# Branch weights moved forward in the sync queue of a hybrid decoder layer with a mixture of experts

## What is computed

```python
xn = rms_norm(x, attn_norm_g)
q, k, v, qi, ki, wi, u, ga, gb = split(xn @ w_in)
attn_o = sparse_attention(...)            # indexer picks keys; sample tokens read paged caches
pool_o = pool_branch(u, ...)
m = sigmoid(ga) * (attn_o @ w_branch_attn) + sigmoid(gb) * (pool_o @ w_branch_pool)
h = x + m @ w_out
h = h + moe_ffn(rms_norm(h, ffn_norm_g))  # 32 experts, each with gate, up and down weights
y = rms_norm(h, final_norm_g)
```

## Time and profile before

| | us |
|---|---|
| three runs | 1102.05, 1099.07, 1102.0; median 1102.0 |
| profiled execution | 1100.63 |
| span in its profile | 1099.1 |
| PE busy | 943.1 (86%) |
| DVE busy | 340.9 (31%) |
| ACT busy | 202.2 (18%) |
| POOL busy | 197.9 (18%) |
| mean DMA rate over the span | 258 GB/s |

### The profile page before, as it was taken

One profiled execution on the slowest core, in us unless ns is written; L12 is line 12 of the kernel. 1 busy time (PEld: TensorE's weight loads), 2 busy tenths in 40 slices (PEclk: granted clock), 3 DMA queues, 4 the chain that ended last, 5 costly groups with the idle time before them and its releaser, 6 DMA issues.

```text
span 1099.1 us, 12164 instructions
## 1 busy us (share of the span) xinstructions
PE 943.1 (86%) x4705; PEld 532.2 (48%) x4705; DVE 340.9 (31%) x756; ACT 202.2 (18%) x446; POOL 197.9 (18%) x296
## 2 busy tenths in 40 slices
PE   7978999999999998999994999888778887878870
PEld 6634444767776656774552434434334242442420
DVE  2269999973441111331226000100000000000016
ACT  3243110213343424000220110000000000000012
POOL 2730660100001110000132111111111111111122
PEclk9989999999999999999996999999999999999995
DMA  9920212512202545933027999999999999999985
GB/s 337 392 86 1 77 47 76 183 53 77 77 1 89 218 154 164 335 149 153 19 96 283 413 421 422 421 423 425 423 422 425 422 425 421 424 425 424 419 320 188
DMA packets 53402, 283.82 MB, mean 258 GB/s; under 512 B 8652, under 2 KB 9520, under 8 KB 32999
## 3 DMA queue, kind: packets, MB, share of 16 engines
q1 hardware_dynamic: 42519, 246.24, 55.8%
q0 software_dynamic: 10784, 36.97, 9.3%
q10 hardware_dynamic: 56, 0.01, 0.0%
HBM read 267.41 MB, written 23.17 MB: 264 GB/s over the span
## 4 chain that ended last, share of the span: by engine, by line
PE 47%; DMA 29%; DVE 18%; ACT 2%; issue 2%; SPq 1%; POOL 0%; ACTq 0%; POOLq 0%; DVEq 0%; PEldq 0%
DMA arena<-in_w_exp_up 24%; PE psum L798 9%; DVE arena L1442 6%; DVE arena L1440 6%; PE psum L952 5%; PE psum L1038 5%; PE psum L934 4%; PE psum L1035 4%; PE psum L1036 3%; PE psum L1053 3%; DMA arena<-in_w_branch_pool 3%; PE psum L622 3%; PE psum L886 1%; DMA y_d<-arena 1%; PE psum L634 1%
## 5 line engine op out<-in xcount | busy, mean ns | idle before, releaser
L1038 PE MATMUL psum<-arena 128*64 128x512 f32 x704 | 169.1, 636 | 30.5 <-DMA arena<-in_w_exp_up 29.8
L1053 PE MATMUL psum<-arena 128*64 128x512 f32 x512 | 116.9, 597 | 17.7 <-ACT arena L1335 17.7
L798 PE MATMUL psum<-arena 128*128 128x288 f32 x480 | 126.1, 416 | 0.0
L1038 PEld LDWEIGHTS psum<-arena 128*64 128x64 f32 x704 | 55.7, 146 | 142.1 <-issue 108.1
L798 PEld LDWEIGHTS psum<-arena 128*128 128x128 f32 x480 | 89.6, 192 | 31.0 <-issue 8.1
L1679 DVE TENSOR_TENSOR arena<-arena,psum 128x256 f32<-128x256 f32 x32 | 13.5, 421 | 277.3 <-ACT arena L1331 277.3
L608 PE MATMUL psum<-arena 128*128 128x512 f32 x192 | 86.2, 604 | 2.1 <-ACT arena L1202 2.1
L1331 ACT ACTIVATE arena<-psum 128x256 f32<-128x256 f32 x32 | 12.3, 383 | 405.1 <-PE psum L1038 277.1
L1053 PEld LDWEIGHTS psum<-arena 128*64 128x64 f32 x512 | 40.4, 136 | 72.1 <-issue 71.4
L1687 DVE COPY arena<-psum 128x512 f32<-128x512 f32 x31 | 21.4, 691 | 152.2 <-PE psum L1053 152.2
L1440 DVE MAX8 arena<-arena 64x8 f32<-64x1032 f32 (+3 forms) x80 | 66.2, 828 | 2.8
(11 more groups left out here) (279 smaller groups left out, 1021.4 us busy)
## 6 DMA issues: line engine op xcount, KB each, us to landing
arena<-in_w_exp_down SPq DMA_DIRECT2D x32, 2048.0 KB, 37.0
arena<-in_w_exp_gate SPq DMA_DIRECT2D x30, 2048.0 KB, 32.7
arena<-in_w_exp_up SPq DMA_DIRECT2D x20, 2048.0 KB, 37.2
arena<-in_w_exp_up SPq DMA_DIRECT2D x24, 1024.0 KB, 34.6
arena<-in_w_in SPq DMA_DIRECT2D x7, 2048.0 KB, 8.7
y_d<-arena SPq DMA_DIRECT2D x1, 8192.0 KB
arena<-in_x_prompt SPq DMA_DIRECT2D x8, 512.0 KB, 7.0
arena<-in_w_out SPq DMA_DIRECT2D x2, 2048.0 KB, 10.9
```

The source lines that it names most:

```text
L798: last = pe.matmul(bank(2 + n % 2 if n < SAMPLE_G else 2, HN), ring[slot % 2][:, k, m * P:(m + 1) * P], xnT[:, k, HN * hh:HN * hh + HN], s ...
L1038: last = pe.matmul(bank(2 + s, 512, rows).rearrange("p (w n) -> p w n", w=2), x_k, wgu[j][:, :, DE * k + 256 * q:DE * k + 256 * q + 256], ...
L1053: last = pe.matmul(bank(4 + s, 512, slice(64 * half, 64 * half + 64)), hT[s][:, k % 2, CAP * (k // 2):CAP * (k // 2) + CAP], wd[j][:, k, 5 ...
```

## The change

Block 7 is issued before the wait for the attention, with only its own wait (`g_done` 24) ahead of it. Block 8 takes the place behind `att_all` and `stores_done`, ahead of the residual's rows, the router's weights and expert 0, where it waits for `g_done` 32. It is taken out from behind expert 0. Nothing else is changed: the other four engines have the same instructions in the same order.

```diff
             for n in range(4, 7):
                 load_ring(n)
 
+            load_ring(7)
             sp.wait_ge(S["att_all"], 1)
             stores_done(sp)
-            load_ring(7)
+            load_ring(8)
             sp.wait_ge(S["gs_done"], len(gb_raw))
             for i in range(TILES):
                 sp.dma_start(resid[0:rows_of(i), i, :], x_rows[i]).then_inc(s_res, 16)
...
             load_gate_up(0, 0)
             load_down(0, 0)
-            load_ring(8)
             sp.dma_start(flat(wg2), g_v[2]).then_inc(s_gu[2], 16)
             load_ring(9)
             load_ring(10)
```

## The result

| | before | after |
|---|---|---|
| median of five runs, us | 1099.75 (1098.78 to 1102.05) | 1094.42 (1092.54 to 1094.63) |
| ratio, 95% interval | | 0.9944 (0.9930 to 0.9958) |
| span in the profile, us | 1099.1 | 1090.9 |
| first L927 to first L952, us | 75.81 | 71.17 |

The changed kernel is faster by 0.56%, with an interval of 0.42 to 0.70%; the medians are 5.3 us apart. The forecast was 4.1 us (0.37%), and 1097.2 us: the direction was right, the measured time lies at the low edge of the range, and the forecast gain lies outside the interval of the ratio.

What follows compares the result with a forecast made beforehand. No engine was taken to bound the whole span (chain 47% PE, 29% DMA, 18% DVE). Two waits, -1.8 - 2.3 = -4.1 us, gave 1097.2 us, the middle of 1096.5 and 1097.9; range 1094.0 to 1100.5.

Steps and rivals of the forecast that it cites:

- Both waits go: PE's idle time before the two branch halves, 1.80 us for block 7 and 2.31 us for block 8, disappears.
- its 442 to 456: Bounds in us for the landing of the moved block 8, which PE wants at 463.8.
- The sum, -1.8 - 2.3: The waits for block 7 and block 8 before the branch halves go, together -4.1 us.
- The upper bound of the forecast, 4.3: Largest gain, -4.3 us: PE's instruction groups overlap by 0.1 us where nothing waits, two times.
- its rivals: Experts swallow the gain, 0.09; only block 7 helps, 0.03; gathers late, kernel slower, 0.03; SP late to block 7, 0.02.
- Block 7 beside the gathers, cost 0: Block 7's 2.1 MB run beside the attention's gathers from 357; cost 0 to 0.5 us, taken as 0.
- the lower bound: Gathers and block 7 share 390 GB/s: values there at 367.1, keys at 372.5, both early, cost 0.
- The upper bound (block 7 whole and first, keys 8.1 us later): Block 7 takes 9.8 us first: values at 372.1, 0.5 us late; keys at 378.5, in time.
- The row that I leaned on: Profile row of DMA slices: in every full slice of a gather the engines reach 344 GB/s and more.
- a gather late by 5.4 us: Estimate for the value gather beside block 7, 2.1 MB at 390 GB/s, within its slack of 9.3 us.
- Everything behind block 8 on SP has room: Residual's rows, router's weights and expert 0 go out 6.9 us later, block 9 comes behind; cost 0.
- The gain is kept by the experts: The expert weights' stream starts and ends as much earlier as PE, so the 4.1 us stay.

Runs made afterwards that it cites:

- the stops: Changed kernel with seven stops of PE put into the branch products: long stops (about 2 us) 1110.91 us, short stops (about 0.5 us) 1099.65 us.
- its repetition: The changed kernel once more with no edit, against the kernel before on the same chip: 1094.04 us, ratio 0.9950.
- block 8 alone: Kernel before with only block 8 moved, to right after block 7, which stays behind the wait for the attention: 1097.35 us, ratio 0.9973.
- block 7 alone twice: Kernel before with only block 7 moved ahead of the attention's wait, profiled twice: 1098.62 us, ratio 0.9987.
- the one with more traffic: Changed kernel with two more transfers of 2 MB issued right behind block 7: 1099.52 us.
- the one with the rest held longer: Changed kernel with residual's rows, router's weights, expert 0 and expert 2's gate weights held until 8 of 32 branch products are done: 1092.82 us, ratio 0.9933.
- the three further profiles: The kernel before, unedited, profiled three more times on another chip: L927 to L952 took 79.72, 76.26 and 76.28 us.

## Why the prediction was right in its mechanism and short in its size

**Both waits go.** Right, in every profile of the changed kernel. Block 8's last transfer was issued at 433.01 and landed 8.4 us later, at 441.4; L927 came 2.2 us earlier than in the kernel before, so this is 443.6 by the forecast's clock, near the lower end of its 442 to 456.

**The sum, -1.8 - 2.3.** This is the step that failed. The mechanism was right and the term was mis-sized: I took the idle time ahead of two instructions, in one execution, for the whole price of a wait. Taken from five profiles of the kernel before and, for the restart, from the stops, the price of the two waits has three parts. The idle time is 2.00 + 2.48 = 4.48 us. The restart is 2 x 0.27 = 0.54 us, which also stands in the first pair of profiles: 2 x 31.31 - 62.08. The clock falls behind four of ten waits, for 1.7 us each: 0.4 x 2 x 1.7 = 1.36 us. Together 6.4 us, and the direct difference of the stretch is 77.50 - 71.17 = 6.3 us. The third part is the least certain, since it comes from two executions of five. The timed runs agree: the mean of the changed kernel's eleven runs (the first five and the six of its repetition) is 1094.07, that of the 53 runs of the kernel before that stood beside the changed ones is 1099.92, so 5.9 us, with a 95% interval of about 0.8 to either side. That excludes the 4.1 of the forecast, and the 4.6 that the first pair of profiles gives. The upper bound of the forecast, 4.3, had taken the overlap of 0.1 us where nothing waits, but neither the full restart nor a granted clock that can fall, since both waits of the one profile stood at 1.00. The forecast named the granted clock nowhere in its rivals. The time itself, 1097.2, had a second error of 1.4 us: it stands on a kernel before of 1101.3 us (1097.2 + 4.1), taken from three runs and one profile, where the 53 runs give 1099.92.

**Block 7 beside the gathers, cost 0.** PE had no new wait there, so the cost was 0, but the delay of the keys was misjudged. The value gather landed at most 9.1 us after its issue instead of 8.0, so the load hardly touched it. The key gather landed after at most 13.0 instead of 7.6 us, 5.4 us later; the lower bound had allowed 2.1 us. The upper bound (block 7 whole and first, keys 8.1 us later) held. The row that I leaned on, the full slices of a gather, is not the rate that this load moves at. Slices of 1 us from 350 to 390 us in the changed kernel, which answer to the earlier trace rows:

```profile
GB/s 0 0 0 115 180 393 369 352 383 385 256 215 234 215 231 324 395 475 356 473 389 401 152 14 0 66 246 401 393 360 393 205 41 16 221 401 410 262 377 311
```

From 360 to 364 only 215 to 256 GB/s are moved, with block 7 and gathers both under way. Block 7 alone had such slices in the kernel before too, where I put them down to its own issuing; here all its transfers had been issued by 358.4, so that was not the reason. Nor is it the gathers. The kernel before, 424 to 474 us in 40 slices of 1.25 us, where no gather runs:

```profile
GB/s 0 66 288 220 226 259 388 392 410 416 410 416 213 312 91 188 133 406 446 419 446 419 419 419 400 433 426 419 282 215 236 213 269 388 495 419 419 419 341 395
```

Block 7 has slices of 220 to 288 from 426.5 on, and block 8 has 213 to 282 from 459 to 465, long after its last issue at 446.81. Its four transfers of `w_branch_attn` landed in these slices, between 461.7 and 465.2. So the low rate goes with these four transfers, with gathers beside them or without; what in them makes it is not separated. By an estimate from these rates their 1.05 MB cost some 2 us more than at 390 GB/s.

The estimate that the forecast made beside the Trainium skill (DMA: Bandwidth & Descriptors, Issuing engines are not separate DMA queues) was a gather late by 5.4 us. The trace has a gather late by 5.4 us, but it is the keys' and not the values'. That the size came out so well is in part luck: the rate was not 390 throughout, and slices that had stood nearly empty between the gathers (57 and 0 in the earlier trace rows) took up a part of the load. A load set beside gathers is not free, and here only their slack hid it.

**Everything behind block 8 on SP has room.** Right. The residual's rows went out at 433.65, as forecast once the earlier start of L927 is taken off, and 12 us more cost nothing that can be seen.

**The gain is kept by the experts.** Right. From L952 to the first L1022 both kernels take 94.8 us, and the stretch of the experts scatters by 1 us in both directions between profiles of one program.

**What stays open.** The 2.17 us by which L927 came earlier in the first pair of profiles arise at about 240 us, long before the first instruction that the change moves. There PE waits for DVE, and the clock fell behind that wait in the profile of before (L798 x16 in 5.84 us) and not in the one of after (4.15 us):

```profile
240.52 0.49 PE L814 MATMUL psum<-arena 64*128 64x128 f32 x4 [2.66 <-DVE arena L1493]
240.94 5.84 PE L798 MATMUL psum<-arena 128*128 128x288 f32 x16
```

```profile
240.04 0.49 PE L814 MATMUL psum<-arena 64*128 64x128 f32 x4 [1.34 <-DVE arena L1493]
240.46 4.15 PE L798 MATMUL psum<-arena 128*128 128x288 f32 x16
```

It fell there in all five profiles of the kernel before, and with block 8 alone. It did not fall in four of the kernels with block 7 moved (the change twice, block 7 alone twice), nor in the one with more traffic, but it fell in the one with the rest held longer and in both with stops. At this place the length of the wait tells the two apart: 2.09 to 2.74 us in the nine profiles with a fall, 1.34 to 2.00 us in the five without. So the fall came in six of six profiles without block 7's move, and in three of eight with it. No run shows how a load at 355 us could shorten a wait at 240, and it may be chance, but that isn't proved. At 1.7 us for each fall these shares would make about 1.1 us of the timed gain. The timed difference, 5.9 give or take 0.8 us, does not decide between 6.3 us of the branch stage alone and the idle time and restart there (5.0 us) with 1.1 us from this place.

## What to carry to other kernels

Price a short wait on TensorE as its idle time plus the restart (0.27 us here, at stops of 0.43 and of 1.80 us) and a chance of slow clock behind it, which was 1.7 us here at waits of 1.86 us and more. Look at the granted clock in steps of 1 us behind each wait, and at more than one profile of the same program: the five here range from 75.8 to 79.7 us in the same stretch. When a difference of a few microseconds is to be forecast, the idle time of one profile was too little here for what its removal gave, 4.1 against 5.9 us. A transfer moved forward into a stretch with other transfers can delay them (the key gather's landing went from 7.6 to 13.0 us): compare their landing time with the moment they are wanted, before and after.

## What was not expected of the hardware

In the branch products the granted TensorE clock fell to half behind stops of 1.86, 2.04, 2.11, 2.32, 2.41, 2.68 and 3.22 us, and did not behind stops of 1.80, 1.85, 1.99, 2.08, 2.31, 2.48 and 2.59 us, nor behind any of 0.43 to 0.75 us. So near 2 us the length of a stop does not decide it there, though at the wait at 240 us all from 2.09 us on had a fall and none up to 2.00 us. The fall comes between the restart itself (at 470.3 us in the first of the three further profiles) and 1.6 us behind it (at the wait at 240 us in the second), and it lasts about 3 us, for a loss of 1.7 us.

In the kernel before, while the four 256 KB transfers of block 8's `w_branch_attn` landed, the DMA engines moved 213 to 282 GB/s, from 459 to 465 us, long after their last issue and without a gather. The slices next to these have 419 and 388 GB/s.
